# A recurrent mixer's input projection in seven block products, with its elementwise work in two halves

## The reference, cut to what matters

```
proj = u @ w_in + b_in                      # 1024 -> 2 * 1280
ybr = gelu(proj[:, :1280])
xbr = causal_dwconv(proj[:, 1280:], conv_w, conv_b)      # 4 taps
gx = sigmoid(xh @ w_gx + b_gx)              # one 128x128 product per row block
ga = sigmoid(xh @ w_ga + b_ga)
log_a = 8 * ga * log_sigmoid(lam)
a_t, mult = exp(log_a), sqrt(-expm1(2 * log_a))
h = scan(h * a_t + mult * gx * xbr)         # over the 256 tokens
out = (h * ybr) @ w_out + b_out
```

## Time and profile before

| | us |
|---|---|
| median of 3 runs | 2385.93 |
| lowest, highest | 2384.86, 2388.27 |
| the profiled execution | 2385.78 |
| its span on the core | 2383.7 |
| mean granted clock of TensorE | 0.931 of full |

### The profile page before, as it was taken

The page is one execution under the profiler, slowest core; times in us unless marked ns, Lnnn a source line. Parts: engine busy times, 40 slices in busy tenths (PEclk is TensorE's granted clock), DMA queues, the critical chain, the costliest instruction groups (busy, mean ns, idle before and its releaser), DMA issues. The chain is left out here.

```text
span 2383.7 us, 29630 instructions
## 1 busy us (share of the span) xinstructions
PE 2085.1 (87%) x12260; PEld 1433.3 (60%) x12260; DVE 1153.5 (48%) x2261; ACT 430.2 (18%) x886; POOL 3.7 (0%) x17
## 2 busy tenths in 40 slices
PE   7999999997666676666766689999999999999998
PEld 5787888862222222222222248878999458899953
DVE  6999897331000011010101128565877756587774
ACT  2232211220000000000000012351333014233311
POOL 0000000000000000000000000000000000000000
PEclk9999999998777878777888899999999999999999
DMA  8526545789999999999999996443454443444530
GB/s 297 198 71 229 161 142 212 268 373 428 428 427 428 428 428 429 427 429 429 428 429 427 428 406 217 165 154 123 170 177 166 177 139 123 177 165 163 177 141 18
DMA packets 149451, 643.75 MB, mean 270 GB/s; under 512 B 10406, under 2 KB 54991, under 8 KB 120927
## 3 DMA queue, kind: packets, MB, share of 16 engines
q1 hardware_dynamic: 148062, 636.76, 67.9%
q10 hardware_dynamic: 1280, 5.44, 0.6%
HBM read 641.10 MB, written 1.08 MB: 269 GB/s over the span
## 5 line engine op out<-in xcount | busy, mean ns | idle before, releaser
L1667 PE MATMUL PS<-arena,hT 128*32 128x512 f32 x2048 | 310.2, 747 | 161.0 <-DMA arena<-in_w_up_dram 118.5
L1667 PEld LDWEIGHTS PS<-arena,hT 128*32 128x32 f32 x2048 | 65.0, 125 | 381.7 <-DMA arena<-in_w_up_dram 191.8
L2129 DVE TENSOR_TENSOR arena<-arena 128x1024 f32<-128x1024 f32 (+2 forms) x283 | 232.3, 841 | 47.6 <-PE PS L2003 23.1
L1721 PE MATMUL PS<-arena,hT 128*32 128x512 f32 x1008 | 171.5, 818 | 88.1 <-DMA arena<-in_w_down_dram 81.0
L1304 PE MATMUL PS<-hT,arena 128*128 128x256 f32 (+1 forms) x1136 | 247.5, 380 | 0.7 <-DMA arena<-in_w_in_dram 0.7
L2126 DVE SCALAR_TENSOR_TENSOR arena<-arena 128x512 f32<-128x512 f32 (+2 forms) x514 | 246.5, 549 | 0.8
L2129 DVE TENSOR_TENSOR hT<-hT,PS 128x512 f32<-128x512 f32 x16 | 16.4, 1026 | 468.1 <-PE PS L1667 468.1
L1304 PEld LDWEIGHTS PS<-hT,arena 128*128 128x128 f32 (+1 forms) x1136 | 210.5, 189 | 32.4 <-issue 2.8
L1202 PE MATMUL PS<-arena 128*128 128x256 f32 (+1 forms) x864 | 188.2, 377 | 0.0
L1202 PEld LDWEIGHTS PS<-arena 128*128 128x128 f32 x864 | 160.4, 190 | 22.5 <-issue 1.7
L1959 PE MATMUL PS<-hT,arena 128*128 128x128 f32 x1408 | 164.9, 275 | 0.7 <-DVE hT L2129 0.7
(11 more groups left out here) (337 smaller groups left out, 2271.3 us busy)
## 6 DMA issues: line engine op xcount, KB each, us to landing
arena<-in_w_gate_dram SPq DMA_DIRECT2D x64, 2048.0 KB, 40.6
arena<-in_w_up_dram SPq DMA_DIRECT2D x64, 2048.0 KB, 40.8
arena<-in_w_down_dram SPq DMA_DIRECT2D x63, 2048.0 KB, 38.4
arena<-in_ffn_w_up_dram SPq DMA_DIRECT2D x32, 2048.0 KB, 8.2
arena<-in_w_in_dram SPq DMA_DIRECT2D x36, 1024.0 KB, 7.9
arena<-in_ffn_w_down_dram SPq DMA_DIRECT2D x16, 2048.0 KB, 7.8
arena<-in_w_ada_dram SPq DMA_DIRECT2D x12, 2048.0 KB, 12.0
arena<-in_ssd_w_in_dram SPq DMA_DIRECT2D x10, 2048.0 KB, 9.8
```

The source lines that it names most:

```text
L1667: mm = pe.matmul(PS[32 * f:32 * f + 32, 1 + half, :], xe[:, 32 * (2 * pi + k):32 * (2 * pi + k) + 32], w[:, k, 512 * f:512 * f + 512], sta ...
L1721: mm = pe.matmul(PS[32 * q:32 * q + 32, 4 + n, :], htr[:, P * q + 32 * pi:P * q + 32 * pi + 32], w[:, q, 512 * n:512 * n + 512], start=(pi ...
L2129: return dve.tensor_tensor(o, a, b, f)
```

## The change

The 16 tiles behind the first four are grouped by four, one panel of weights a group (`L_GROUPS = 4`). Each group is a 2x2 block product with blocks of four input blocks by two output tiles of weights and of four input blocks by 128 tokens of the input, and is made in seven products of eight 128x128 matmuls (`l_product`). The four sums of weight blocks (`l_weight_sums`) go into a ring slot of their own for each group: `TAIL` has four entries `lru_sum` that load nothing. The sums of input blocks (`l_acts`) are made once, ahead of `raw_scale`. ScalarE copies between chained products, four times a group, with the bias in the same instruction, in two pieces of 128 columns (`l_chain_copy`: `l_p1`, `l_u2`, `l_u3`, `l_c21`). VectorE adds three parts a group (`l_part_11`, `l_part_22`, `l_part_12`). Two of the x tiles and two of the y tiles stand in group 1; groups 2 and 3 are y tiles. The gate products use three PSUM banks instead of four. Decays, products, roots, scans and `times_y` run for the row blocks 0 to 4 first and for 5 to 9 after them, and the gelu is taken of six y tiles and then of four.

```diff
@@ stream of weight panels @@
-TAIL = [("ssd_x", 1), ("ssd_dt", 1), ("ssd_x", 5), ("ssd_z", 4), ("ssd_out", 4), ("ffn0", 24), ("lru_in", 5),
-        ("lru_g", 1), ("lru_out", 3), ("ffn1", 24)]
+TAIL = [("ssd_x", 1), ("ssd_dt", 1), ("ssd_x", 5), ("ssd_z", 4), ("ssd_out", 4), ("ffn0", 24), ("lru_in", 2), ("lru_sum", 1),
+        ("lru_in", 1), ("lru_sum", 1), ("lru_g", 1), ("lru_in", 1), ("lru_sum", 1), ("lru_in", 1), ("lru_sum", 1), ("lru_out", 3), ("ffn1", 24)]
...
@@ ScalarE @@
-            for t in range(NL):
-                c = COL["lru_b_in_2"] + NL + t
-                if t < 4:
-                    act.wait_ge(s["raw_ev"], 4 * PRE.index("mix_pre1") + t + 1)
-                    src = pads[:, t, 3:3 + T]
-                else:
-                    act.wait_ge(*tile_done(s, used, "ly_ps", ["lru_in"], t - 3))
-                    act.wait_ge(s["lcv_done"], t - 3)
-                    src = PS[:, t % 4, 0:T]
...
+            def l_chain_copy(n, g, dst, half, scale):
+
+                act.wait_ge(s["chain_ps"], CHAIN + n)
+                for u in range(2):
+                    ins = act.activation(dst[:, u, :], PS[:, g % 2, P * u:P * u + P], ACT.Identity,
+                                         bias=l_bias(4 * (g + 1) + 2 * half + u), scale=scale)
+                ins.then_inc(s["chain_ev"], 1)
...
+            for t in range(4):
+                act.wait_ge(s["raw_ev"], 4 * PRE.index("mix_pre1") + t + 1)
+                act.activation(pads[:, t, 3:3 + T], pads[:, t, 3:3 + T], ACT.Identity, bias=l_bias(t)
+                               ).then_inc(s["ly_ready"], 1)
+                if t == 0:
+                    l_p1(0)
+                if t == 2:
+                    l_u2(0)
+            l_u3(0)
+            l_p1(1)
+            l_c21(0)
+            gate_pair(0)
+            l_u2(1)
+            gate_pair(2)
+            l_u3(1)
+            l_p1(2)
+            l_c21(1)
+            gate_pair(4)
+            gate_pair(6)
+            l_u2(2)
+            gate_pair(8)
+            l_u3(2)
...
+            for h in range(4):
+                decay(h)
+            l_p1(3)
+            decay(4)
+            l_c21(2)
+            for h in range(5):
+                decay_root(h)
+                if h == 2:
+                    l_u2(3)
...
+            act.activation(yb[:, 0:L_EARLY_Y, :], yb[:, 0:L_EARLY_Y, :], ACT.Gelu_apprx_tanh).then_inc(s["ly_ready"], 1)
+            l_u3(3)
+            for h in range(5, NL):
+                decay(h)
+                if h == 6:
+                    l_c21(3)
+            for h in range(5, NL):
+                decay_root(h)
...
+            act.activation(yb[:, L_EARLY_Y:NL, :], yb[:, L_EARLY_Y:NL, :], ACT.Gelu_apprx_tanh).then_inc(s["ly_ready"], 1)
@@ TensorE @@
-            for m in range(4, 2 * NL):
...
-                mm = tile(PS[:, n, 0:T], [(w[:, k, P * n:P * n + P], hs[:, k, :]) for k in range(KD)],
-                          norm=None if m > 4 else "mix_pre1")
...
+            def l_product(bank, weights, acts, opens_bank, ready=None, gates_done=0):
+
+                for u in range(2):
+                    for k in range(4):
...
+                        mm = pe.matmul(PS[:, bank, P * u:P * u + P], weights[:, k, P * u:P * u + P], acts[:, k, :],
+                                       start=(opens_bank and u == 0 and k == 0), stop=(k == 3), skip_group_check=True)
...
+            def l_s1t1(n):
+
+                if n == 0:
+                    pe.wait_ge(s["t_sums"], T_SUMS + 1)
+                l_product(2 + n % 2, l_weights(n, "t1"), s_sum[0], True)
+
+            def l_s2t2(n):
+
+                pe.wait_ge(s["t_sums"], T_SUMS + 2)
+                pe.wait_ge(s["chain_ev"], CHAIN + max(4 * n, 1))
+                l_product(n % 2, l_weights(n, "t2"), s_sum[1], False).then_inc(s["chain_ps"], 1)
...
+            def l_last(n):
+
+                pe.wait_ge(s["t_sums"], T_SUMS + 4)
+                pe.wait_ge(s["part_add"], 3 * N_SPLIT + 3 * n + 2)
+                l_product(2 + n % 2, l_weights(n, "b22"), s_sum[3], False
+                          ).then_inc(used, ST.incs["lru_in"][n + 1] + ST.incs["lru_sum"][n])
+
+            l_first(0)
+            for n in range(L_GROUPS):
+                pe.wait_ge(s["l_sums"], n + 1)
+                if n >= 2:
+                    pe.wait_ge(s["part_add"], 3 * N_SPLIT + 3 * n - 3)
+                if n < L_GROUPS - 1:
+                    l_s1t1(n)
+                    if n:
+                        lru_gates((0, 6)[n - 1])
+                    l_s2t2(n)
+                    l_second(n)
+                    if n:
+                        lru_gates((2, 8)[n - 1])
+                    l_s3t3(n)
+                    l_first(n + 1)
+                    l_fourth(n)
+                    if n == 1:
+                        lru_gates(4)
+                else:
+                    l_s2t2(n)
+                    l_s1t1(n)
+                    l_s3t3(n)
+                    l_second(n)
+                    l_fourth(n)
+                l_last(n)
@@ VectorE @@
+            def l_weight_sums(n):
...
+                link("mix_tmp", tt(t[:, 0:4, :], b11, b12, ALU.add))
+                link("mix_tmp", tt(t[:, 4:8, :], t[:, 0:4, :], b22, ALU.add))
+                tt(t[:, 8:12, :], b12, b22, ALU.add)
+                tt(t[:, 12:16, :], t[:, 4:8, :], b21, ALU.add).then_inc(s["l_sums"], 1)
...
+                tt(s_sum[0], a22, a21, ALU.subtract).then_inc(s["t_sums"], 1)
...
+                stt(s_sum[1], s_sum[0], -1.0, a11, ALU.mult, ALU.subtract).then_inc(s["t_sums"], 1)
+                tt(s_sum[2], a11, a21, ALU.subtract).then_inc(s["t_sums"], 1)
...
+                stt(s_sum[3], a12, -1.0, s_sum[1], ALU.mult, ALU.subtract).then_inc(s["t_sums"], 1)
...
+            l_acts()
+            raw_scale("mix_pre1", "lru_in", lambda n: pads[:, n, 3:3 + T], rstd[:, :])
+            for t in range(4):
+                l_conv(t)
+            l_weight_sums(1)
+            dve.wait_ge(s["lcv_done"], 4)
+            l_part_11(0)
+            l_part_22(0)
+            l_part_12(0)
+            for t in range(4, 8):
+                l_conv(t)
+            dve.wait_ge(s["lcv_done"], 6)
+            l_part_11(1)
+            l_part_22(1)
+            l_weight_sums(2)
+            l_part_12(1)
+            l_conv(8)
+            l_conv(9)
...
+            for h in range(5):
+                decayed(h)
+            for h in range(4):
+                scanned(h)
+            l_part_11(3)
+            l_part_22(3)
+            scanned(4)
+            for h in range(5):
+                times_y(h)
+            for h in range(5, 8):
+                decayed(h)
+            l_part_12(3)
+            for h in range(8, NL):
+                decayed(h)
+            for h in range(5, NL):
+                scanned(h)
                 times_y(h)
```

More of the change, by code:

```diff
@@ L175, in __init__ @@
         for name, n in TAIL:
-            for j in range(n):
+            for i in range(n):
+                j = len(self.pos.get(name, [])) if name in ("lru_in", "lru_sum") else i
                 if name in ("ffn0", "ffn1"):
@@ L180, in __init__ @@
                 else:
-                    put(name, TAIL_SLOT[(nxt + j) % RING_TAIL], p, 2 if (name, j) in TWO_LOADS else 1)
+                    loads_of = 2 if (name, j) in TWO_LOADS else 0 if name == "lru_sum" else 1
+                    put(name, TAIL_SLOT[(nxt + i) % RING_TAIL], p, loads_of)
                 p += 1
@@ L443, in program @@
         hs = view(arena, S6 + 17408, KD, T)
+        l_kept = [view(arena, S6 + 19456 + T * i, 2, P) for i in range(4)]
         rfin, var = (arena[:, S6 + 19456 + T * i:S6 + 19712 + T * i] for i in range(2))
@@ L2064, in lru_gate @@
                 pe.wait_ge(s["lcv_done"], h + 1)
-                if h >= 4:
-                    pe.wait_ge(s["lsig"], 2 * (h - 3))
-                pe.matmul(PS[:, 4 + h % 4, 0:T], slot(g, NL, P)[:, h, :], xb[:, h, :], start=True, stop=True)
-                return pe.matmul(PS[:, 4 + h % 4, T:512], slot(g, NL, P, NL * P)[:, h, :], xb[:, h, :],
+                if h >= 3:
+                    pe.wait_ge(s["lsig"], 2 * (h - 2))
+                pe.matmul(PS[:, 5 + h % 3, 0:T], slot(g, NL, P)[:, h, :], xb[:, h, :], start=True, stop=True)
@@ new lines, in l_s3t3, with l_fourth @@
+            def l_s3t3(n):
+                pe.wait_ge(s["t_sums"], T_SUMS + 3)
+                pe.wait_ge(s["chain_ev"], CHAIN + 4 * n + 2)
+                l_product(n % 2, l_weights(n, "t3"), s_sum[2], False, None,
+                          ST.incs["lru_g"][0] if n == 2 else 0).then_inc(s["chain_ps"], 1)
+            def l_fourth(n):
+                pe.wait_ge(s["chain_ev"], CHAIN + 4 * n + 3)
+                l_product(n % 2, l_weights(n, "t4"), hs[:, 4:8, P:T], False).then_inc(s["chain_ps"], 1)
@@ L2850, in ffn_dve @@
                 wc = COL["ffn_conv_w_2"] + 192 * layer
-                chain, sums = CHAIN * layer, T_SUMS * layer + 4
```

(11 more changed lines are left out.)

195 lines of the change are left out of this document (125 added, 70 removed).

## The result

The changed kernel takes 2391.58 us (median of 11 runs, 2390.03 to 2393.9), the one before 2386.34 in the same comparison (11 runs, 2384.86 to 2388.27). The ratio is 1.0023, 95% interval 1.0015 to 1.0031: slower by 5.2 us, a little over the 0.2% that count as a difference here. The interval lies wholly above 1 and reaches to both sides of the 0.2%. The profiled execution took 2390.03 us, its span 2388.0 (2383.7 before), at a mean granted clock of 0.933 (0.931).

What follows compares the result with a forecast made beforehand. TensorE was taken as the bound. Stops 8.1 us, clock 1.65, products -5.2 and the 0.12 gap gone gave +4.4 us on the profiled execution's 2385.78, that is 2390.2 us, range 2387.0 to 2394.5.

Steps and rivals of the forecast that it cites:

- small stops: TensorE's short waits at the end of group 2 and in group 3, for VectorE's part and ScalarE's copies: 1.7 us.
- Products: TensorE's projection: 28 products of 1.79 us, 50.1 us in place of 55.3, so 5.2 us less.
- First stop: TensorE, after its first product, waits for VectorE's input sum `s_sum[0]`: 0.6 us.
- second: TensorE waits for ScalarE's first chain copy, queued behind the first tile's bias, which waits for `raw_scale`: 1.7 us.
- Third: Group 0's last product waits for `l_part_22(0)`, behind convolutions and group 1's sums on VectorE: 4.1 us.
- The clock: TensorE's clock falls to 1.2 GHz once, behind its 4.1 us wait in group 0: 1.65 us, bounds 0 and 3.3.
- Rival 1: The clock does not fall behind the wait in group 0, or that wait is shorter: 2388.6 us; chance 0.16.
- Sums that are hidden: Group 0's weight sums, 4.8 us, fit into VectorE's 7.01 us wait for the norm and cost nothing.
- The end of the mixer: VectorE ends about 2050.0, TensorE wants the tenth row block about 2051.2; cover about 1 us, priced at nothing.
- rival 2: VectorE becomes the bound; sign: `lh_ready` wait before L1612 or over 1 us in group 3; 2392.0 to 2394; chance 0.26.
- Rival 4: Each of seven ScalarE table loads holds it another 1.28 us: +10.4 us, 2396.2; chance 0.02.
- Rival 3: The saving is kept, VectorE reaching `l_part_22(0)` before TensorE does: -1.3 us, 2384.5; chance 0.04.

Runs made afterwards that it cites:

- e1_warm: Changed kernel plus eight idle matmuls in TensorE's wait ahead of group 0's last product: 2390.06 us, 1.0016 of the kernel before.
- e2_p1_first: Changed kernel with ScalarE's first chain copy `l_p1(0)` ahead of the first tile's bias: 2393.05 us, 1.0030 of the kernel before.
- e6_whole: Changed kernel with decays, roots and scans of all ten row blocks together and one gelu of ten tiles: 2400.52 us, 1.0063 of the kernel before.
- e4_two_early: Changed kernel with two of group 1's weight sums before the norm, group 0's parts ahead of the other two: 2385.92 us, 0.9997 of the kernel before.
- e5_order: On e4_two_early: ScalarE's chain copies ahead of bias, decays, roots, gelu; VectorE's parts between sums and scans: 2386.33 us, 0.9995 of the kernel before.
- e7_raw_first: On e4_two_early: `raw_scale` ahead of the last two input sums, `l_second` before `l_s2t2` in group 0: 2385.89 us, 0.9999 of the kernel before.
- e8_both: e7_raw_first with the group 3 order of e5_order added: 2385.19 us, 0.9995 of the kernel before.
- e3_parts_first: Changed kernel with group 0's parts `l_part_11(0)` and `l_part_22(0)` ahead of group 1's weight sums: 2391.55 us, 1.0020 of the kernel before.

## Why the prediction was right, and where it was off

The forecast was +4.4 us on the profiled execution; that execution came out +4.25, the stretch +4.77, the medians +5.2. So the mechanism was right and its size nearly so. I gave "same" 0.52 and "slower" 0.46; the 0.18% that I forecast measured 0.23%, and the line of 0.2% between the two lies inside the interval. That the profiled execution met the forecast to 0.2 us is luck: its mixer began 0.86 us earlier than the one before, and by the medians 0.8 us are missing in the forecast. The largest of them are the small stops (0.3), the passes behind a stop (0.25) and the wait behind the stretch (0.36), which I had not looked at.

*Products.* 1.785 us each (32 passes in 3.57), forecast 1.79. *First stop* 0.67, forecast 0.6; *second* 1.71, forecast 1.7. *Third* 4.00, forecast 4.1: with the start of the projection set equal, VectorE ends the part at 1987.52 (1986.66 + 0.86), forecast 1987.6; TensorE is there at 1983.67, forecast 1983.5. Nine products stand ahead of the first gate, as expected.

*The clock.* 1.70 us, forecast 1.65, and 0.50 granted behind the stop as in the earlier trace rows; e1_warm priced it alone at 1.63. The agreement has luck in it: I took the price from one block of 16 passes in another loop, and it fits because the granted clock stayed at 0.50 for about 3.4 us in both places (my estimate from windows of one microsecond); behind the longer stops of e2_p1_first and e6_whole it cost 2.16 and 2.84. The Trainium skill ("TensorE: Matmul & The Clock Gate", "Why this matters for your kernels") was right in speaking against gaps. Rival 1, that the clock would not fall, is refuted.

*Small stops.* Here is the term that was mis-sized. The forecast has 1.7 us in all (0.4, 0.2, 0.6, 0.4, rounded up); measured are 0.70 ahead of `l_last(2)`, 0.68 ahead of `l_s3t3(3)` and 0.64 ahead of `l_fourth(3)`, 2.02. The 0.2 us for `l_p1(3)` did not come, since the stop before it had grown. Besides, the first sixteen passes behind a stop take longer to the next product, 1.86 us from 2028.89 to 2030.75 and 1.89 from 2033.18 to 2035.07, which with those at 1973.80 makes 0.25 us that I did not have. The gap ahead of the output product, 0.12 us in the chain of the earlier trace rows, has to be read start to start like the rest. TensorE's timeline of the kernel before has

```profile
2011.88 20.88 PE L1202 MATMUL PS<-arena 128*128 128x256 f32 x96
2032.88 14.05 PE L2098 MATMUL PS<-arena 128*128 128x256 f32 x64
2046.77 20.88 PE L1538 MATMUL PS<-arena 128*128 128x256 f32 x96
```

Six tiles take 20.73 us from start to start, so the gap was 0.27 us, and the first four row blocks took 13.89 us where they now take 13.82. Together: stops 8.40 + clock 1.70 + 0.25 - products 5.30 - gap 0.27 - 0.07 = 4.71, where the stretch has 4.77.

*Sums that are hidden.* VectorE idles 2.23 us for the norm, forecast some 2, after four sums in 4.87 us (forecast 4.8). They cost nothing. The step that I did not take is that these 2.23 us were nearly free for two more sums: with the parts ahead of the other two, that is e4_two_early, 5.6 us.

*The end of the mixer.* VectorE ends at 2049.84, which is 2050.70 with the starts set equal, forecast 2050.0; TensorE wants it at 2050.68. The cover was 0.84 us, forecast about 1, and no wait stands ahead of L1612. The point from which rival 2 decides, VectorE losing more than 1 us, was not reached: it lost 0.7. But group 3's waits are 1.3 us in all, which is over the 1 us that I named as its sign. That sign was badly chosen: both are waits for copies that stand behind other work of ScalarE, and e5_order takes them away, though 1.56 us stand in that run ahead of `l_last(3)` and of the output product. What is true in rival 2 is that VectorE is a second bound in the first group, and e5_order, e7_raw_first and e8_both show it; the price forecast for it, 1.8 us more, was not paid.

*Table loads.* Rival 4 is refuted. ScalarE's timeline:

```profile
2029.84 1.28 ACT L1241 ACT_TABLE_LOAD   x1
2031.13 1.48 ACT L1241 ACTIVATE arena<-arena 128x1536 f32<-128x1536 f32 x1
```

The next ACTIVATE starts 1.29 us behind the load's start, as in the earlier trace rows, and so it does behind the five other loads of the mixer that have work waiting; the 2.66 us of the Trainium skill ("ScalarE: Activation LUTs", "What ACT_TABLE_LOAD costs") are not met here either.

Rival 3, the saving kept, was wrong: the sums of group 1 took their 4.87 us and stood in the way. Its number is another matter: with the third stop taken away in e4_two_early the stretch is 0.9 us under that of before, near the -1.3 that I worked out for it. What stays open is whether e5_order or e8_both is faster as a whole: both ratios are 0.9995, and the intervals reach to both sides of 1.

## What to carry to other kernels

Trading TensorE's matmuls for VectorE's sums is worth what VectorE's list allows: lay the lists beside each other, find the instruction on which TensorE waits, and ask what of the work queued ahead of it is not needed yet and which idle time could take it. Here two sums moved into an idle time of 2.2 us, and two parts taken ahead of the other two sums, turned +4.8 us in the stretch into -0.9. Take away the stop that the lagging engine sets, not one in front of it: 1.7 us saved ahead of such a wait came back but for 0.16, and once in full with a longer spell at the low clock.

## What the runs showed of the hardware that I had not expected

The clock fell behind a shorter stop than I had allowed for. By the brackets of the timelines, in the changed kernel 1.48 us left it full, as 1.88 did before; in e3_parts_first 2.06 us brought it down, with TensorE busy without a gap from 1977.48 to its start (windows, columns as in the earlier trace rows):

```profile
1988.00:1990.00 2.00, 0.43 (x4) 0.24 (x3) 1.97 (x3) 0.67 (x1) 0.00 (x0) 1.00 0.29 27
1990.00:1992.00 2.00, 1.50 (x8) 1.50 (x9) 1.93 (x5) 0.00 (x0) 0.00 (x0) 0.73 0.93 321
1992.00:1994.00 2.00, 2.00 (x10) 2.00 (x10) 1.89 (x5) 0.00 (x0) 0.00 (x0) 0.50 1.05 410
```

In e2_p1_first, with a stop of 5.54 us, it fell while TensorE still stood:

```profile
1984.00:1986.00 2.00, 0.00 (x0) 0.00 (x0) 1.97 (x3) 0.13 (x1) 0.00 (x0) 0.80 0.00 0
1986.00:1988.00 2.00, 0.36 (x2) 0.39 (x3) 1.49 (x3) 0.00 (x0) 0.00 (x0) 0.50 0.00 0
```

So halving a stop need not save the clock's part, and the price is not a constant. With the stops counted start to start it was 1.70 us behind 4.00 us, 1.74 behind 2.23 (1990.50 to 1994.89 in e3_parts_first, 4.39 us for 2.65), 2.16 behind 5.70 (e2_p1_first, 5.73 us for 3.57), 2.84 behind 7.2. The profile in windows of one microsecond shows what the price is made of: it is half of the time in which TensorE works at the low clock. By my estimate from them that is 3.4 us in the changed kernel (1987.5 to 1990.9) and in e3_parts_first (1990.9 to 1994.3), 4.4 in e2_p1_first (1987.64, where TensorE starts, to 1992.0) and 5.6 in e6_whole (2044.74 to 2050.3). Why the clock stays low longer behind the two longest stops, and why 2.06 us brought it down where 1.88 had not, these runs do not settle.
